# Moving cache copies, two waits and two loads in a decode-step kernel on one core

## What is computed

```python
q, k, v, u = split_mix_proj(rmsnorm(x, g_mix), w_in)
o_a = merge(dilated attention (128,1), (512,4), (2048,16))   # prompt: own keys; sample: cache + own keys
o_b = pool_mix(u, ...)
x = x + concat(o_a, o_b) @ w_out
x = x + cross_attn(rmsnorm(x, g_x), mk, mv)    # prompt: mk, mv from mem_prompt; sample: cache_mem_k, cache_mem_v
x = x + moe(rmsnorm(x, g_ff), ...)             # top 4 of 32 experts, all 32 experts' weights are streamed
y = rmsnorm(x, g_final)
k_win_sample = concat(cache_k_win, k)[:, 4:]   # 8 x 2044 rows of old cache go out again, the same for v
```

## Time and profile before

| | |
|---|---|
| median of 3 runs | 1411.29 us (1403.95 to 1412.52) |
| the profiled execution | 1409.75 us, of which the span 1408.0 |
| TensorE busy | 1255.7 us (89%) |
| VectorE, ScalarE, GpSimd busy | 481.2, 230.3, 67.7 us |
| moved by DMA | 557.14 MB, mean 396 GB/s |
| mean granted TensorE clock | 0.968 of full speed |

### The profile page before, as it was taken

How to read it: one execution, slowest core, us unless ns; L and a number is a source line. 1 busy time by engine, 2 the same in 40 slices (tenths; PEclk the granted TensorE clock), 3 DMA queues, 4 the chain that set the end, 5 groups by cost and what they waited for, 6 DMA issues and landing times.

```text
span 1408.0 us, 16530 instructions
## 1 busy us (share of the span) xinstructions
PE 1255.7 (89%) x6407; PEld 528.5 (38%) x6407; DVE 481.2 (34%) x1037; ACT 230.3 (16%) x448; POOL 67.7 (5%) x69
## 2 busy tenths in 40 slices
PE   7989877989897999998999989999899998999986
PEld 5444323456644433333333333333333333333332
DVE  2387888332326412312232122321223212132124
ACT  1334443211311110110110100110011010011102
POOL 2010000005007000000000000000000000000000
PEclk9999988999997999999999999999999999999998
DMA  9999999998989699999999999999999999999993
GB/s 339 353 381 363 399 397 379 361 370 306 360 354 344 254 431 427 427 429 426 429 428 429 429 429 429 428 430 427 430 427 430 427 429 428 429 429 429 429 428 158
DMA packets 51740, 557.14 MB, mean 396 GB/s; under 512 B 7021, under 2 KB 9301, under 8 KB 15885
## 3 DMA queue, kind: packets, MB, share of 16 engines
q1 hardware_dynamic: 50629, 553.04, 96.0%
q0 software_dynamic: 1072, 3.57, 0.6%
HBM read 552.02 MB, written 71.72 MB: 443 GB/s over the span
## 4 chain that ended last, share of the span: by engine, by line
DMA 55%; PE 35%; DVE 5%; ACT 2%; issue 1%; SPq 1%; DVEq 0%; ACTq 0%; PEldq 0%
DMA wide<-in_w_gate_up 49%; PE bank L1954 12%; DMA wide<-in_cache_v_win 3%; PE bank L1642 3%; PE bank L1983 2%; PE bank L1684 2%; PE bank L1749 2%; PE bank L1512 2%; PE bank L1508 1%; PE bank L1662 1%; DMA slim<-in_w_xq 1%; DMA slim<-in_w_xv 1%; ACT wide L787 1%; PE bank L1737 1%; PE bank L1791 1%
## 5 line engine op out<-in xcount | busy, mean ns | idle before, releaser
L1954 PE MATMUL bank<-wide,att 128*64 128x512 f32 x2048 | 463.3, 596 | 58.5 <-DMA wide<-in_w_gate_up 58.3
L1954 PEld LDWEIGHTS bank<-wide,att 128*64 128x64 f32 x2048 | 139.3, 136 | 362.5 <-issue 228.8
L1983 PE MATMUL bank<-slim,att 128*64 128x512 f32 x1024 | 226.8, 595 | 0.0
L1422 DVE TENSOR_SCALAR att<-bank 128x512 f32<-128x512 f32 x32 | 22.1, 691 | 469.0 <-PE bank L1954 469.0
L1983 PEld LDWEIGHTS bank<-slim,att 128*64 128x64 f32 x1024 | 70.6, 137 | 152.2 <-issue 149.2
L1401 DVE TENSOR_TENSOR x<-x,bank 128x512 f32<-128x512 f32 x68 | 46.6, 685 | 233.1 <-PE bank L1936 226.4
L980 ACT ACTIVATE att<-att 128x512 f32<-128x512 f32 x32 | 20.2, 630 | 517.6 <-DVE att L1422 517.6
L1936 PE MATMUL bank<-tb,att 128*128 128x512 f32 (+1 forms) x192 | 84.7, 611 | 1.8 <-ACT tb L989 1.3
L989 ACT ACTIVATE tb<-bank 64x512 f32<-64x512 f32 x64 | 37.8, 591 | 234.1 <-PE bank L1983 233.7
L1662 PE MATMUL bank<-slim,ta 128*128 128x512 f32 x128 | 57.8, 601 | 0.5 <-DMA slim<-in_w_xv 0.3
L1176 DVE TENSOR_REDUCE small<-wide 128x24 f32<-128x1536 f32 x28 | 49.1, 1753 | 1.0
(11 more groups left out here) (290 smaller groups left out, 1153.1 us busy)
## 6 DMA issues: line engine op xcount, KB each, us to landing
wide<-in_w_gate_up SPq DMA_DIRECT2D x128, 2048.0 KB, 25.4
slim<-in_w_down SPq DMA_DIRECT2D x64, 2048.0 KB, 22.0
out_k_win_sample<-in_cache_k_win SPq DMA_DIRECT2D x16, 2044.0 KB, 25.3
out_v_win_sample<-in_cache_v_win SPq DMA_DIRECT2D x16, 2044.0 KB, 22.9
wide<-in_w_in SPq DMA_DIRECT2D x8, 1024.0 KB, 15.8
wide<-in_cache_v_win SPq DMA_DIRECT2D x8, 1024.0 KB, 7.5
wide<-in_cache_mem_k SPq DMA_DIRECT2D x8, 1024.0 KB, 24.4
wide<-in_cache_mem_v SPq DMA_DIRECT2D x8, 1024.0 KB, 14.7
```

Source lines behind the costliest of these rows:

```text
L1954: ins = M(bk[half[h], :], rows[:, k, :], wide[:, k, c:c + 512], start=False, stop=k == KC - 1)
L1983: ins = M(bank_y[half[h], :], aT[:, f % 4, f // 4, :], slim[:, f, 512 * h:512 * h + 512], start=f == 0, stop=f == KC - 1)
```

## The change

Five edits:

- COPIES is another list with the same places: one copy more at the front, one less after the last loads of w_xk and in each of sample steps 2, 4, 5 and 6; one more in cross-attention and one more after the router weights. The sum falls from 31 to 29, so 3 pieces and no longer 1 are left for the place between step0 and the loop.
- The loads of the identity and of x tile 1 are issued by ScalarE, ahead of its first wait, and no longer by SP.
- VectorE's wait for late_k goes from ahead of the rows into row(b, 0), just ahead of the product with the ninth slot.
- TensorE's wait for late_v goes from the head of values() to its first matmul with the ninth slot, and the kinds are taken in the order 0, 1, 2, 3.
- The toep matmul goes ahead of the ten bias matmuls.

```diff
-        COPIES = [5, 1, 3, 1, 2, 2, 2, 2, 2, 2, 3, 2, 1, 3]
+        COPIES = [6, 1, 2, 1, 1, 1, 1, 1, 2, 2, 4, 2, 2, 3]
...
+        ident_rows, second_rows = i["c_ident"], i["x_prompt"][0, P:2 * P, :]
...
         def _(sp):
-            load(sp, "ident", ident[:, :], i["c_ident"])
-            for t in (0, 2, 1):
+            for t in (0, 2):
...
+            load(act, "ident", ident[:, :], ident_rows)
+            load(act, "x1", x[:, 1, :], second_rows)
             act.wait_ge(consts, 2)
...
                 if b:
...
                     V.tensor_tensor(pd[:, 0:2, :], pair, ps[:, :].unsqueeze(1).broadcast_to([P, 2, AW]), ALU.mult)
+                    if t == 0:
+                        dve.wait_ge(late_k, b + 1)
                     V.tensor_tensor(pd[:, 2, :], kw[:, 8, :], ps[:, :], ALU.mult).then_inc(s, 1)
                 else:
...
+                    if t == 0:
+                        dve.wait_ge(late_k, 1)
                     V.tensor_tensor(pd[:, 2, :], late_first, ps[:, :], ALU.mult).then_inc(s, 1)
...
             dve.wait_ge(k_in[0], 64)
-            dve.wait_ge(late_k, 1)
...
             dve.wait_ge(k_in[1], 64)
-            dve.wait_ge(late_k, 2)
...
                 dve.wait_ge(k_in[b % 2], 64 * (b // 2 + 1))
-                dve.wait_ge(late_k, b + 1)
...
+            ps, s = take(pe, "toep")
+            M(ps[0:HEADS, 0:TOEP], rb, cb[:, 0:TOEP], start=True, stop=True).then_inc(s, 1)
             for kind in range(6):
...
-            ps, s = take(pe, "toep")
-            M(ps[0:HEADS, 0:TOEP], rb, cb[:, 0:TOEP], start=True, stop=True).then_inc(s, 1)
...
                 pe.wait_ge(v_in, 64 * (b + 1))
-                pe.wait_ge(late_v, b + 1)
                 ps, s = take(pe, "pv", b)
...
-                for k, kind in enumerate((2, 0, 1, 3)):
+                for k, kind in enumerate((0, 1, 2, 3)):
+                    if kind == 2:
+                        pe.wait_ge(late_v, b + 1)
                     for t in range(DEC_T):
```

## The result

The changed kernel takes 1411.0 us (median of 20 runs, 1408.42 to 1416.64), the kernel before 1407.5 (20 runs, 1402.61 to 1412.52). The ratio is 1.0031, 95% interval 1.0018 to 1.0044: slower by 2.5 to 6.2 us, where the forecast had 2 us gained. The outcome is that of the third rival, the front copy that is paid, though not by the condition written there.

A forecast was written before the change was run, and what follows sets the result against it. The expert weight stream, DMA-bound at 428 GB/s, was untouched, so only the 470 us ahead counted: 0 (start) + 0 (front copy) - 2.7 + 0.7 = -2.0 from 1409.75, so 1407.75, rounded 1408; range 1400 to 1415.

The forecast's parts named there:

- the third rival: Front copy paid: sample 1's key window 5.5 us late, values(1) follow if value window lands with its issue; 1413.3, chance 0.2.
- The start: Kernel start: ScalarE's issues and the earlier toep matmul save up to 3.3 us (1.7 by the skill's rule); counted 0, swallowed.
- Where that gain stops: Sample 1's key window: sixth front copy delays its first product 5.5 us (0 to 6.5), swallowing the start's 3.3.
- Where that loss stops: Sample 1's value window: same bytes ahead, lands at 138.7 us, its wait hides the delay; 0, bounds -0.6 and +1.7.
- The faster values(1): Values of sample 1, without idle in front, may take 2.78 us for 24 matmuls instead of 5.05, giving the excess back.
- values(1) at about 142: Sign expected in the changed profile: values of sample 1 still start at about 142 us.
- its bound on the window, 3 us either way: Sign of being wrong: sample 1's value window moves by more than 3 us either way.
- The sample steps: Samples 3 on: waits for late rows go, values(4) to (6) released by shares, 20.0 us apart; -2.7 us, bounds 0 and 8.8.
- Cross-attention and loop entry: Moved copies mostly fill idle DMA time in cross-attention and before step 1's loads; +0.7 us, range 0 to +5.
- One sign of being wrong: Expert loop entry: step 1's first w_gate_up piece lands more than 3 us later against step 0's start.

The follow-up runs named there:

- the run that moved one copy alone: Kernel before with one copy moved from the third COPIES entry (sample 1's step) to the first, all else untouched: 1412.98 us, ratio 1.0045.
- four in front of the kernel before: Kernel before with front COPIES entry 4 in place of 5 and one copy more in sample 2's step: 1414.93 us, ratio 1.0055.
- before, second: The kernel before run once more, unchanged, for a second profile: 1407.46 us.
- four in front of either kernel: Front entry 4 in the kernel before (ratio 1.0055), or in the changed kernel with one copy more in sample steps 4, 5 and 6 (1398.39 us, 0.9947).
- three: Changed kernel with front entry 3 and one copy more in each of sample steps 2, 4, 5 and 6: 1398.11 us, ratio 0.9936.
- one piece left over: Changed kernel with two of the three copies at the loop's entry put back into sample steps 5 and 6: 1411.17 us, ratio 1.0026.
- the old list: Changed kernel with the old COPIES list, so only the start and the waits are new: 1405.51 us, ratio 0.9981.
- list alone: Kernel before with the new COPIES list alone: 1412.87 us, ratio 1.0050.
- five in front: Changed kernel with five copies at the front, not six, the sixth put into sample step 6: 1405.04 us, ratio 0.9982.
- start alone: Kernel before with ident and x tile 1 issued by ScalarE and the toep matmul ahead of the ten bias matmuls: ratio 0.9993.
- waits alone: Kernel before with late rows awaited at their slot and kinds of late values third in order: ratio 1.0001.
- the first four experiments: The list alone in the kernel before; the changed kernel with the old list, with one piece left over, with five in front: ratios 1.0050, 0.9981, 1.0026, 0.9982.

## Why the prediction was wrong, step by step

**The start** was under-sized: 5.6 us instead of 3.3 at line 1508, since TensorE, which no longer paused, also ran the first small matmuls faster (0.81 us for the two of the toep product, 1.44 in before); the reason is not shown. That it is swallowed by the key window is right: with five copies in front the window lands at 93.0 to 93.6 us whether the start is early or not, and TensorE waits 3.24 to 5.75 us for it in the three kernels with the early start. The Trainium skill ("DMA: Bandwidth & Descriptors", section "Issuing engines are not separate DMA queues") states that a second issuer saves issue time alone. By the forecast that is 0.9 us here. In three of the six profiles with the old start TensorE waits 0.71, 0.97 and 1.16 us for x1, which 0.9 us would take away nearly or wholly; in the other three it waits 2.16 to 2.55, of which 1.3 to 1.7 would be left. None stands in the seven kernels profiled with the new start. So in half of the profiles the trace goes beyond the rule; either way the time was swallowed.

**Where that gain stops** is right: window forecast 5 to 6 us late, 6.09 measured (99.73 against 93.64), SP's queue full.

**Where that loss stops** is the step that failed. It let the delay end in the wait for sample 1's value window and took 0, with bounds of -0.6 and +1.7; measured are +4.35 and +4.17 at values(1).
- Only idle time hid the delay. In all thirteen profiles values(1) start at the later of two times: 21.4 us behind values(0), which is work without a pause (21.41 or 21.42 in the ten profiles without a wait there, after and the run that moved one copy alone among them), or 3.4 us behind the landing of the window (before, its second profile, and four in front of the kernel before). In before the landing decides, by 4.05 us: values(1) stood 25.54 us behind values(0), the other 21.49 are work. A delay at values(0) eats those 4.05 us, and all the rest goes through. The forecast had the 4.05 too. By its delay of 5.5 it left 1.45 over, and by its upper bound of 6.5 it would have been 2.45, more than the 1.7 it gives. The 16.72 us that the window took, less 7.5, hid nothing beyond the 4.05.
- The queue did not stay full either (DMA share 0.57 in 126 to 130 us, last row of the first table below): the window was issued later and landed earlier than in before, so the forecast's landing at 138.7 and the rival's landing that moves with its issue were both wrong, and neither decided. A window that lands later than the work needs it does decide, as that of sample 2 with four in front of the kernel before.
- The delay was under-sized. Forecast 5.5; measured 6.08 at the first broadcast and 8.47 at values(0). Between the two lie 19.61 us in before and 22.00 in after, and this goes with TensorE's clock. The table of stretches (us; busy of PE, PEld, DVE, ACT, POOL; PEclk; DMA share; GB/s), first of after, then of before:

```profile
90.00:103.00 13.00, 0.58 (x2) 0.00 (x0) 0.00 (x0) 3.19 (x6) 0.00 (x0) 0.65 1.00 411
95.00:100.00 5.00, 0.00 (x0) 0.00 (x0) 0.00 (x0) 0.25 (x1) 0.00 (x0) 0.50 1.01 406
103.00:116.00 13.00, 10.37 (x44) 7.88 (x45) 8.86 (x14) 10.14 (x29) 2.85 (x4) 0.69 1.03 416
126.00:130.00 4.00, 4.00 (x31) 1.17 (x24) 3.90 (x6) 3.60 (x8) 0.00 (x0) 1.00 0.57 217
```

```profile
90.00:103.00 13.00, 10.41 (x42) 5.34 (x40) 8.74 (x16) 7.17 (x13) 3.30 (x5) 1.00 0.98 362
103.00:116.00 13.00, 11.71 (x46) 6.49 (x46) 8.09 (x11) 9.96 (x31) 0.54 (x1) 1.00 1.03 402
```

  TensorE stood idle for 12.47 us, the granted clock fell to 0.50, the lower of its two levels, and was on average 0.69 in the 13 us behind; in before it was 1.00. In the second profile of before it was 0.87 there and the distance 20.94 us. The thirteen profiles, by the granted clock from the first broadcast of sample 1 to values(0):

| granted clock | broadcast to values(0), us | kernels (TensorE's idle time ahead of the broadcast, us) |
|---|---|---|
| 1.00 | 19.61 | before (0.43) |
| 0.92 | 20.94 to 21.16 | before, second (0.28); four in front of either kernel, three (0) |
| 0.82 | 21.92 to 22.00 | after (12.47), one piece left over (12.62), the old list (5.75) |
| 0.71 to 0.77 | 22.20 to 23.20 | list alone (7.25), one copy moved (7.30), five in front (5.54), start alone (3.24), waits alone (1.78) |

  So the distance goes with the clock, and not with the length of the wait. After lost 0.8 to 1.1 us by it against the four profiles at 0.92, and 2.4 against the first profile of before, the only one at full clock. No term of the sum had this.
- The faster values(1) (2.78 us for 24 instead of 5.05) were to give the excess back. They came, and values(2) are only 2.50 us late (164.88 against 162.38). But values(2) then took 4.85 us at a granted clock of 0.57, where before had 2.78 at 1.00, and at values(3) it is 3.29 again.

So 8.47 - 4.05 = 4.4 is the loss at values(1), and by the forecast's own 5.5 it would have been 1.5. Of the forecast's signs on this path "values(1) at about 142" failed; its bound on the window, 3 us either way, held (about 136 against 138.7), since the path did not go by the window. The rival with the right outcome stood at 1413.3 with a chance of 0.2.

**The sample steps** went as described, but were over-sized: line 1152 releases, and the values of samples 4 to 6 are 20.36 and 19.97 us apart. From values(1) to w_out after is 3.3 us shorter than the first profile of before and 1.0 shorter than the second, but part of that is the faster values(1). From values(3) to w_out, where the forecast had -2.7, it is 69.37 us in after, 71.65 in the first profile of before and 69.59 in the second: -2.3 or -0.2. The seven kernels with the new waits need 68.85 to 69.39 us there, the other five profiles of the old ones 69.59 to 70.08. The price came from one execution of before, the only one that long; against the others the edit is worth 0.2 to 1.2 us.

**Cross-attention and loop entry** were sized well enough. From SP's issue of w_xq to the last matmul of line 1954 it is 1086.84 us in before, 1087.07 in after, 1087.76 with one piece left over. In the first four experiments it is 1085.5 to 1089.6, without an order by the pieces left over (1 or 3). Within that sum, after is 2.9 us shorter than before to step 1's first issue (176.15 against 179.08) and 3.2 longer from there (910.92 against 907.76), as if the copies had only changed sides; but the second experiment, with the old list, shows 177.43 and 909.66, so I don't put this down to them. Forecast were +0.7; measured +0.2. One sign of being wrong did show: step 1's first piece lands 17.2 us behind the first matmul of line 1958 (1954 in before), 11.1 in before, 6 us later where the forecast allowed 3; the stretch as a whole shows no such loss. That the toep load is slower than a copy, on which the choice of 0.7 rests, no run shows by itself.

**Sum.** 0 (start), +4.2 to +4.4 (front copy, forecast 0), -1.0 to -3.3 (sample steps and what lies to w_out), +0.2 to +0.3 behind w_xq: +1.2 against the first profile, +3.5 against the second. The first ran 2.2 us above the median of before, the second at it (1407.46 and 1407.5), so the second is the better yardstick: there the front copy costs 4.2 us at values(1) and still 3.4 at values(3) instead of 0, and the waits bring 0.2 instead of 2.7.

## What to carry to other kernels

A transfer queued ahead of an awaited one can cost its full length: 5.88 of 6.25 us here in front, and a gain in front was lost again to a third copy ahead of sample 2's window. It costs little where a row shows that the awaited one has slack, as with three or four copies in front. Before a delay is declared hidden in a later wait, take as what can hide the idle time of the engine that is late, 4.05 us here, not the time that the transfer takes, 16.72. Then carry the delay to that very place, with what the engine loses in clock on the way: 5.5 us were forecast, 8.47 arrived. And price a wait from more than one execution: 2.7 us from the one profile of before were 0.2 by the other. The early start alone gave nothing that can be told, a copy taken from the front and put ahead of the next awaited window lost 0.55%, and the change with two copies fewer in front gained 0.5%; that the early start and the shorter front need one another is likely, but not shown.

## What was not expected of the hardware

One copy of 2.093 MB in front moved the window's landing by 6.25 and 5.94 us (6 to 5 and 5 to 4 copies), which is 335 and 352 GB/s; copies behind a toep load and weights do not go at the 428 GB/s of the experts' stream. And a wait costs more than its length: behind 12.47 us of idle time the 8 turns of line 1553 took 2.04 us at half clock, against 1.13 in both profiles of before (line 1550), and 0.8 to 2.4 us came on top by values(0), by which profile it is held against. The longer wait was not the dearer one: behind 7.30 us of idle time values(0) came 23.08 us later at a mean clock of 0.71, behind 12.47 us 22.00 us later at 0.82.
